# Small constant products ahead of each feed-forward piece, and another filler before them

## The reference, cut to what matters

```python
D_FF = -(-8 * D_MODEL // (3 * 256)) * 256        # 2816 = 11 pieces of 256

    u = rmsnorm(h, ffn_pre_norm[i])
    gate, up = jnp.split(u @ w_gate_up[i], [D_FF], axis=-1)
    y = (jax.nn.silu(gate) * up) @ w_down[i]
    h = h + rmsnorm(y, ffn_post_norm[i])
    h = h + (p[i] @ ple_proj[i]) * jax.nn.sigmoid(h @ ple_gate[i])
```

## Time and profile before

| | |
|---|---|
| median of 3 runs | 1048.36 us |
| lowest, highest | 1045.7, 1054.06 us |
| span of the profiled execution | 1050.0 us |
| TensorE busy in it | 994.2 us (95%) |
| VectorE, ScalarE busy | 626.8 us, 514.3 us |
| mean granted TensorE clock | 0.984 of full speed |

### The profile page before, as it was taken

How to read it: one execution, slowest core, us unless ns; L and a number is a source line. 1 busy time by engine, 2 the same in 40 slices (tenths; PEclk the granted TensorE clock), 3 DMA queues, 4 the chain that set the end, 5 groups by cost and what they waited for, 6 DMA issues and landing times.

```text
span 1050.0 us, 19418 instructions
## 1 busy us (share of the span) xinstructions
PE 994.2 (95%) x8568; PEld 919.7 (88%) x8568; DVE 626.8 (60%) x833; ACT 514.3 (49%) x693; POOL 19.7 (2%) x23
## 2 busy tenths in 40 slices
PE   7999999999999999999996587799999999999998
PEld 6999999899989999997673455499999999999998
DVE  6798789868766875443110110189985755555566
ACT  5576497844675563523110111277666653443453
POOL 0000021001000000000000000000000000000000
PEclk9999999999999999999998988899999999999999
DMA  7665453446245357888999999954323356555531
GB/s 290 246 236 192 170 201 124 168 156 236 81 150 212 139 224 297 315 354 333 420 420 420 421 419 423 394 192 177 139 81 128 119 206 205 196 181 189 193 121 41
DMA packets 34871, 241.74 MB, mean 230 GB/s; under 512 B 4064, under 2 KB 4448, under 8 KB 6368
## 3 DMA queue, kind: packets, MB, share of 16 engines
q1 hardware_dynamic: 33264, 233.32, 58.3%
q0 software_dynamic: 1232, 6.99, 1.9%
q10 hardware_dynamic: 288, 0.15, 0.1%
HBM read 239.36 MB, written 1.08 MB: 229 GB/s over the span
## 4 chain that ended last, share of the span: by engine, by line
PE 76%; DMA 12%; DVE 7%; ACT 2%; SPq 2%; issue 1%; DVEq 0%; ACTq 0%
PE ps L479 18%; PE ps L481 18%; PE ps L480 18%; DMA wr<-in_c_weights 8%; PE ps L568 3%; PE ps L1278 3%; DMA T8b<-in_c_weights 3%; SPq L3053 2%; DVE wlo L2044 2%; PE ps L965 1%; PE ps L1228 1%; DVE xs L2276 1%; ACT whi L1388 1%; PE ps L1305 1%; PE ps L830 1%
## 5 line engine op out<-in xcount | busy, mean ns | idle before, releaser
L2044 DVE TENSOR_TENSOR wlo<-raw,whi 128x2048 fp32r<-128x2048 f32 (+1 forms) x119 | 271.2, 2282 | 113.7 <-ACT whi L1388 113.3
L479 PE MATMUL ps<-XUh,whi 128*128 128x256 f32 x992 | 280.4, 283 | 0.7 <-DVE wlo L2044 0.6
L480 PE MATMUL ps<-XUl,whi 128*128 128x256 f32 x992 | 276.2, 278 | 0.0
L481 PE MATMUL ps<-XUh,wlo 128*128 128x256 f32 x992 | 276.2, 278 | 0.0
L1388 ACT ACTIVATE whi<-raw 128x2048 fp32r<-128x2048 f32 (+1 forms) x119 | 225.0, 1893 | 47.7 <-PE ps L481 41.2
L479 PEld LDWEIGHTS ps<-XUh,whi 128*128 128x128 f32 x992 | 186.5, 188 | 2.7 <-issue 1.7
L480 PEld LDWEIGHTS ps<-XUl,whi 128*128 128x128 f32 x992 | 188.0, 189 | 0.7 <-issue 0.5
L481 PEld LDWEIGHTS ps<-XUh,wlo 128*128 128x128 f32 x992 | 186.2, 188 | 0.0
L2976 DVE SCALAR_TENSOR_TENSOR sphs<-sphs,wsl,ps 128x256 f32<-128x256 f32 x8 | 3.8, 480 | 91.0 <-ACT sphs L2009 71.8
L479 PE MATMUL ps<-ffnah,whi 128*128 128x256 f32 x176 | 49.5, 281 | 0.0
L480 PE MATMUL ps<-ffnal,whi 128*128 128x256 f32 x176 | 49.5, 281 | 0.0
(11 more groups left out here) (624 smaller groups left out, 2372.9 us busy)
## 6 DMA issues: line engine op xcount, KB each, us to landing
raw<-in_c_weights SPq DMA_DIRECT2D x137, 1024.0 KB, 4.9
wr<-in_c_weights SPq DMA_DIRECT2D x36, 1024.0 KB, 26.1
xhi<-in_c_weights SPq DMA_DIRECT2D x12, 1024.0 KB, 26.3
xlo<-in_c_weights SPq DMA_DIRECT2D x12, 1024.0 KB, 26.5
extra<-in_c_weights SPq DMA_DIRECT2D x10, 1024.0 KB, 27.5
T<-in_c_weights SPq DMA_DIRECT2D x5, 1024.0 KB, 26.1
T8b<-in_c_weights SPq DMA_DIRECT2D x5, 1024.0 KB, 26.4
acb<-sums POOLq DMA_DIRECT2D x4, 1024.0 KB, 4.9
```

The costliest lines, as they stand in the source:

```text
L479: pe.matmul(ps, h(k), xh(k), start=start and k == 0, stop=False, skip_group_check=loose)
L480: pe.matmul(ps, h(k), xl(k), start=False, stop=False, skip_group_check=loose)
L481: t = pe.matmul(ps, l(k), xh(k), start=False, stop=stop and k == kt - 1, skip_group_check=loose)
L2044: dve.tensor_tensor(l[:, 0:n], r, h[:, 0:n].bitcast(F32), ALU.subtract).then_inc(*did("w_lo", "split", i))
```

## The change

The filler of 12 products of ones becomes 16 fp32r matmuls on the tile `MIh`, the high part of the operand of the product before: 8 of 512 columns and 8 of 256 columns. And in `ffn_up` each gate and up piece from up 1 on (19 pieces; gate 1 keeps its `lead_in`, and the down pieces get nothing) starts with a small product into its own PSUM bank, which the piece's first matmul clears. Which one depends on the piece, in a turn of five: one transpose, one fp32r matmul of 128 columns, one fp32 product of ones of 128 columns, the `lead_in` of two transposes, one fp32 product of ones of 64 columns.

```diff
-        constant_products(pe, ps[:, 0:128], 12)
+        for k in range(4):
+            pe.matmul(ps[:, :], MIh[:, k, 0:128], MIh[:, 4:6, :].rearrange("p k n -> p (k n)"))
+        for k in range(8):
+            pe.matmul(ps[:, 0:256], MIh[:, k, 128:256], MIh[:, 7 - k, :])
+        for k in range(4):
+            pe.matmul(ps[:, :], MIh[:, 2 + k, 0:128], MIh[:, 4:6, :].rearrange("p k n -> p (k n)"))
...
             if (n, c) == ("gate", 1):
                 lead_in(ps)
+            elif c > 0 and n != "down":
+                m = (2 * c + (n == "up") - 3) % 5
+                if m == 0:
+                    pe.transpose(ps[:, 0:128], ident, ident)
+                elif m == 1:
+                    pe.matmul(ps[:, 0:128], h[:, 0, 0:128], XUh[:, 0, 0:128])
+                elif m == 2:
+                    constant_products(pe, ps[:, 0:128], 1)
+                elif m == 3:
+                    lead_in(ps)
+                else:
+                    pe.matmul(ps[:, 0:64], ones[:, :], ones[:, 0:64])
```

## The result

The changed kernel takes 1054.5 us (median of 6 executions, 1053.25 to 1056.46) where the kernel before took 1047.19 us beside it (6 executions): the ratio is 1.007, with a 95% interval from 1.0048 to 1.0092. It is slower, by less than 1%; the forecast was 1046.4 us with a range up to 1052.5.

A forecast was written before the change was run, and what follows sets the result against it. TensorE's matmul stream was taken to bound the feed-forward stage. A 5.1 us gain from shorter spacing less 3.2 us for small products, filler 0, gave 1.9 us off 1048.36: about 1046.4 us, range 1042 to 1052.5.

The forecast's parts named there:

- The bound and the two spacings: Feed-forward stage: lasts as long as TensorE's matmul stream, spaced 113.4 or 117.8 ns, kept until something else comes between.
- The base: Feed-forward layer: all 1512 matmuls at 117.8 ns, as in the profiled execution of 1050.0 us.
- rival B: Feed-forward stream: long spacing is an accident of the profiled execution, so the change adds 3.2 us, 1051.6 us; chance 0.13.
- 5 of 5 short behind 128-column products: Gate, up and down pieces: 912 matmuls behind transposes, 128-column products and lead-ins turn short, gaining 4.0 us.
- the fp32r and the 64-column kinds: Pieces behind these products: 480 matmuls, nothing alike in the trace, gain between nothing and 2.1 us, taken as 1.05.
- The products' own cost: Small products before 19 gate and up pieces: all on TensorE's path, costing 3.2 us, bounds 2.8 to 4.1.
- The filler: Ahead of gate 0: 2.76 us of new matmuls stay inside the wait for `XP`, costing 0, at most some 0.2 us.
- The formula of the Trainium skill: Matmul stream: one distance per width, N/2.4 + 2.5 ns, so nothing turns and the change costs its small products alone.

The follow-up runs named there:

- the last kernel: New filler and one transpose before up 1 alone, against the kernel before: median 1047.35 us, ratio 0.9953.
- the two-product kernel: One transpose before up 1 and one fp32r matmul before gate 2, old filler, against the kernel before: median 1052.57 us, ratio 1.0045.

## Why the prediction was wrong

**The bound and the two spacings** held. The stage lasts as long as TensorE's stream, the stream has two spacings, it keeps the one it has, and small products change it. TensorE is busy for all 170 us from 842 to 1012 in every profile, so VectorE, ScalarE and the transfers never became the bound there.

**The base** failed, and with it the sign. The sum was made against an execution with all 1512 matmuls long. Seven in ten executions of before have them short, so there was nothing to win in them. This was rival B, which I gave 0.13; its price, the products' 3.2 us, held no matmul that turns long, and so its 1051.6 us was too low as well. Two things misled me. I set the span of 1050.0 against the median of 1048.36 and read 1.6 us between them; a time is 1.8 us more than its span, so that execution stood 3.4 us above the median, in the upper of two groups. And I argued that places of one sort come out alike within a trace. That says nothing of one place in two executions: between the two profiles of the kernel before, the first stream (48 matmuls from 26.58 and 27.57 us), the one behind the mixture of experts, up 0 and the whole feed-forward stream came out differently. The three times of before already had two, 1045.7 and 1048.36, below the empty stretch and one, 1054.06, above it.

**"5 of 5 short behind 128-column products"** failed. It counted kinds, and the kind alone is not what decides. Of the small products behind which I expected 912 matmuls short, the single transpose left a long piece long once in four, and the 128-column product turned a short stream long once in four. The lead-in was short four times of four there and long every third time when it stood everywhere. For the fp32r and the 64-column kinds I had taken half. The fp32r one turned a short stream long in three of three pieces of the changed kernel, and the 64-column one in three of three. In the fourth place the fp32r one came behind a long piece and turned it short. In all, 192 of the 912 came out long, and of the 480 of the two other kinds 432. Even against the execution that the sum was made for, the stage is shorter by 178.05 - 177.71 = 0.3 us and not by 1.9: 888 short matmuls are worth 3.9 us rather than 5.1, and the products cost 3.5 rather than 3.2. Against a short base, 624 long matmuls are a loss of 2.7 us rather than a gain of 5.1.

**The products' own cost** was near: 3.5 us against 3.2. The single term that was mis-sized most is the 64-column product, 0.23 us where I took 0.15: it costs as much as one of 128 columns.

**The filler** was right: 0 us, hidden behind `XP`, and the last kernel confirms it in the times. That it could change how up 0 settles I named, and left out as 48 x 4.4 ns = 0.2 us. But gate 1 had the spacing of up 0 in all 16 profiles, so in a kernel without the small products the term may be as large as 6.7 us. Whether the filler does shift it stays open: the filler alone was in the upper group 10 times in 21 and the kernel before, beside it, 12 times in 64. On one chip it was 5 of 9 against 2 of 26, on another 5 of 10 against 10 of 31, and the second pair doesn't show a difference. In the changed kernel it matters for up 0 and gate 1 alone, since the products draw anew.

**The rest.** From a short base the stage explains 177.7 - 171.3 = 6.4 us, and the medians differ by 7.3. The profile of after is also 1.2 us longer than that of before between the last triple ahead of the mixture of experts and the first behind it, 222.1 against 220.9 us. But the kernel before has both values too, 220.9 in its first profile and 222.1 in its second, so this is no effect of the change. The products alone stood 4.4 us over before and the whole change 7.3, in different comparisons, against bases of 1048.02 and 1047.19. Their profiled executions, 1049.9 and 1052.5 us long, have the same stage, 177.71 us. 1.4 us of the difference lies ahead of the mixture of experts, whose last triple ahead starts at 466.2 and 467.6 us, and 1.2 us in it, 220.9 and 222.1. The kernel before has 466.6 and 467.8 us for the first of these in its two profiles. So this part too looks like one of executions and not of the filler; two profiles can't prove it for the medians.

The formula of the Trainium skill named in the prediction ("TensorE: Matmul & The Clock Gate", "Back-to-back issue gap"), 109 ns at 256 columns, stands there for an isolated matmul, which the prediction left out. Of a stream of weight loads and matmuls the same section says that both operations set the spacing, and it gives one figure for a width there too. With one distance for a width the change would have cost its products alone, 3.5 us, and the sign would have been right. But 624 matmuls in the changed kernel are 4.4 ns further apart than the others of the same width at the same clock, and the two-product kernel has a stage 6.5 us longer than its 0.24 us of products account for.

## What to carry to other kernels

Before a sum is made against one profiled execution, its span plus the constant between span and time should be placed among the timed runs. If these fall into groups, the sum has to say which group the trace is from. A stream of like matmuls can have more than one spacing at the same clock, and what stands before it can change which; over 1500 matmuls that was worth more than anything the small product cost. One short product at the head of a long stream can be enough, if its trace shows which way it turns the stream (the transpose before up 1 was followed by the short spacing in 7 profiles of 7, the fp32r matmul before gate 2 by the long one in 4 of 4), while one before every piece draws again each time and pays each time.

## What was new of the hardware

- Triples of fp32r matmuls, 128x128 by 256 columns, ran at 113.4 or 117.8 ns apart at a granted clock of 1.00, and held either over 1416 matmuls and more.
- With the same transposes before each of 19 pieces of a stream that repeats after three matmuls, what came out was a turn of three with two of them (long, short, short) and with one (short, long, long); with three, 18 of 19 pieces came out alike. Which resource of TensorE has this period isn't shown; no run here looked inside a weight load or a write to PSUM.
- A stream that starts behind the same code came out short or long from one execution to the next, with shares of the upper group of times from 0 of 7 to 15 of 23 on different chips. What differs between these isn't shown. The spacing outlived a sum of plain fp32 matmuls and two transposes: gate 1 had that of up 0 in 16 profiles of 16.
- A plain fp32 product of 64 columns cost 0.23 us inside the stream, as much as one of 128 columns, and a single transpose or a single fp32r matmul of 128 columns 0.12 us.
